# A hybrid layer on one core: group squares joined on VectorE, an addition moved ahead of a silu, and one page group read by two queues

## The reference, cut to what matters

```python
def _gated_group_rmsnorm(y, z, w, out_dtype):
    g = y.astype(jnp.float32) * jax.nn.silu(z.astype(jnp.float32))
    shp = g.shape
    g = g.reshape(*shp[:-1], SSD_GROUPS, D_INNER // SSD_GROUPS)
    g = g * lax.rsqrt(jnp.mean(g * g, axis=-1, keepdims=True) + RMS_EPS)
    return (g.reshape(shp) * w.astype(jnp.float32)).astype(out_dtype)
```

```python
        k_past = cache_k[layer, pt].reshape(past, KV_HEADS, hd)
        v_tail = cache_v[layer, pt[own_start // PAGE_SIZE:]].reshape(-1, KV_HEADS, hd)
```

## Time and profile before

| | us |
|---|---|
| median of 3 runs | 1838.3 (1833.46 to 1839.65) |
| the profiled execution's own time | 1838.51 |
| its span, first to last instruction | 1836.8 |
| TensorE busy | 1755.9 (96%) |
| its weight loads busy | 1620.0 (88%) |
| VectorE busy | 934.1 (51%) |
| GpSimd busy | 955.8 (52%) |
| ScalarE busy | 614.5 (33%) |
| mean granted TensorE clock | 0.981 |

### The profile page before, as it was taken

One profiled execution on the slowest core, in us unless ns is written; L12 is line 12 of the kernel. 1 busy time (PEld: TensorE's weight loads), 2 busy tenths in 40 slices (PEclk: granted clock), 3 DMA queues, 4 the chain that ended last, 5 costly groups with the idle time before them and its releaser, 6 DMA issues.

```text
span 1836.8 us, 35809 instructions
## 1 busy us (share of the span) xinstructions
PE 1755.9 (96%) x13948; PEld 1620.0 (88%) x13948; DVE 934.1 (51%) x1552; ACT 614.5 (33%) x1652; POOL 955.8 (52%) x1090
## 2 busy tenths in 40 slices
PE   6999999999999999999898999999998999999987
PEld 6888988999889999776676998779998999999987
DVE  6776677641765423666465632212246661562463
ACT  4355545422544200455343112321024430331231
POOL 4544434455443466220453634226676886776774
PEclk9999999999999999999999999999999999999998
DMA  4213222223123223111796364632221322222222
GB/s 160 70 49 105 95 83 70 99 66 118 58 95 101 79 91 125 47 47 58 254 310 209 137 195 175 224 116 95 86 81 59 92 81 81 81 81 93 80 71 107
DMA packets 53478, 198.50 MB, mean 108 GB/s; under 512 B 6353, under 2 KB 7378, under 8 KB 49746
## 3 DMA queue, kind: packets, MB, share of 16 engines
q1 hardware_dynamic: 41330, 132.83, 22.7%
q10 hardware_dynamic: 7200, 47.81, 6.9%
q0 software_dynamic: 4800, 15.73, 2.5%
HBM read 180.43 MB, written 15.92 MB: 107 GB/s over the span
## 4 chain that ended last, share of the span: by engine, by line
PE 82%; DVE 5%; ACT 4%; issue 3%; DMA 3%; POOL 2%; POOLq 0%; DVEq 0%; SPq 0%; ACTq 0%
PE dps L221 64%; PE psLE L1595 1%; DVE cout L850 1%; DMA w_raw<-wstream_dram 1%; DMA pages<-kv_pages_dram 1%; PE psY L586 1%; PE psY L1332 1%; POOL w_lo L2510 1%; PE psY L1618 1%; ACT cs_rhs L645 1%; PE psY L522 1%; PE psLE L2040 1%; PE psLE L2002 1%; PE psA L1322 1%; PE psLE L572 1%
## 5 line engine op out<-in xcount | busy, mean ns | idle before, releaser
L2510 POOL TENSOR_TENSOR w_lo<-w_raw,w_hi 128x256 fp32r<-128x256 f32 x804 | 678.1, 875 | 16.8
L2506 POOL TENSOR_SCALAR w_hi<-w_raw 128x1024 fp32r<-128x1024 f32 x201 | 219.4, 1092 | 708.8 <-PE dps L221 691.3
L221 PE MATMUL dps<-xn_hi,w_hi 128*128 128x288 f32 x2160 | 479.5, 304 | 12.8 <-DVE xn_lo L323 4.5
L221 PE MATMUL dps<-xn_lo,w_hi 128*128 128x288 f32 x2160 | 466.0, 298 | 0.0
L221 PE MATMUL dps<-xn_hi,w_lo 128*128 128x288 f32 x2160 | 465.9, 298 | 0.0
L221 PEld LDWEIGHTS dps<-xn_hi,w_hi 128*128 128x128 f32 x2160 | 353.8, 192 | 43.2 <-issue 28.6
L221 PEld LDWEIGHTS dps<-xn_lo,w_hi 128*128 128x128 f32 x2160 | 352.4, 191 | 0.0
L221 PEld LDWEIGHTS dps<-xn_hi,w_lo 128*128 128x128 f32 x2160 | 351.5, 191 | 0.0
L221 PE MATMUL dps<-y_hi,w_hi 128*128 128x288 f32 x896 | 194.2, 299 | 5.4 <-POOL w_lo L2510 5.4
L221 PE MATMUL dps<-y_lo,w_hi 128*128 128x288 f32 x896 | 193.0, 297 | 0.0
L221 PE MATMUL dps<-y_hi,w_lo 128*128 128x288 f32 x896 | 192.9, 297 | 0.0
(11 more groups left out here) (383 smaller groups left out, 2605.3 us busy)
## 6 DMA issues: line engine op xcount, KB each, us to landing
w_raw<-wstream_dram SPq DMA_DIRECT2D x217, 512.0 KB, 3.5
pages<-kv_pages_dram SPq DMA_DIRECT2D x68, 256.0 KB, 3.8
pages<-kv_pages_dram POOLq DMA_DIRECT2D x60, 256.0 KB, 4.0
st_in<-state_t_dram ACTq DMA_DIRECT2D x8, 1024.0 KB, 4.8
ssm_s_dram<-st_in ACTq DMA_DIRECT2D x8, 1024.0 KB, 5.0
kc<-mem_kt_dram ACTq DMA_DIRECT2D x4, 2048.0 KB, 7.8
vc<-mem_v_dram ACTq DMA_DIRECT2D x3, 2048.0 KB, 7.9
h_res<-x_t_dram ACTq DMA_DIRECT2D x1, 2304.0 KB, 8.8
```

Source lines behind the costliest of these rows:

```text
L221: mm = pe.matmul(dps[:, par, b, 0:cw], w, a[:, k, c0:c0 + cw], start=(k == 0 and j == 0), stop=(k == nk - 1 and j == 2))
L2506: pool.tensor_scalar(w_hi[:, par, :], w_raw[:, par, :], 1.0, 1.0, ALU.mult, ALU.mult).then_inc(w_hi_done, 1)
L2510: ins = pool.tensor_tensor(w_lo[:, par, at], w_raw[:, par, at], w_hi[:, par, at].bitcast(F32), ALU.subtract)
```

## The change

Three things are changed.

1. The ten one-column products of `pe_gsum` become five: `dve_squares_joined` on VectorE first adds the squares of the group's second 128 features to those of the first, in place. `gsq_ready` now counts two for each group. `pe_gsum` also moves behind the next group's first chunk, except in group 4, where it stays in front of the output tiles, and group 7, which has no such chunk.
2. In `dve_slot`, `dve_round` comes ahead of `dve_silu` in slots 2 to 5.
3. Page group 3 is read two pages by SP and two by GpSimd, when `pv_full` says that the last products of the prompt's attention are done, and no longer behind `sam_start`. Both read its page numbers ahead of that wait. SP's weight load for the stage's next gate tile moves ahead of it too. SP's two pages are counted on `kv_landed[8]`, which is what the counts in `pages_here` take into account.

GpSimd has two of the four reads left, behind pv_full. The diff:

```diff
--- before.py
+++ after.py
@@ -578,12 +578,11 @@
 
         def pe_gsum(pe, G):
 
-            pe.wait_ge(gsq_ready, G + 1)
+            pe.wait_ge(gsq_ready, G * 2 + 2)
             pe.wait_ge(y_free, G * 5 + 5)
             for c in range(CH + 1):
                 at = slice(c * P, c * P + P) if c < CH else slice(T - P, T)
-                for j in range(2):
-                    mm = pe.matmul(gsum[:, c:c + 1], xg_of(G)[:, j, at], ones[:, 0:1], start=(j == 0), stop=(j == 1))
+                mm = pe.matmul(gsum[:, c:c + 1], xg_of(G)[:, 0, at], ones[:, 0:1], start=True, stop=True)
             mm.then_inc(gsum_full, 1)
 
         def pe_grow(pe, G):
@@ -621,14 +620,16 @@
                         pe_round(pe, G, k - 2)
                     if k < 5:
                         pe_chunk_out(pe, G, k)
-                    else:
-                        pe_gsum(pe, G)
                     if k < 4:
                         pe_chunk(pe, G, k + 1)
+                    if k == 5 and out_tiles(G, k):
+                        pe_gsum(pe, G)
                     for m in out_tiles(G, k):
                         pe_dense(pe, MIXER_AT["out", 0, m], y_hi, y_lo, ready=counted(glo_ready, 1) if m == 0 else None)
                     if k == 5 and G < GROUPS - 1:
                         pe_chunk(pe, G + 1, 0)
+                    if k == 5 and not out_tiles(G, k):
+                        pe_gsum(pe, G)
 
 
         def act_rhs(act, G, s):
@@ -878,6 +879,12 @@
             dve.tensor_tensor(zg_of(G), yg[:], zg_of(G), ALU.mult).then_inc(gate_ready, 1)
             dve.wait_ge(gate_ready, G + 1)
 
+        def dve_squares_joined(dve, G):
+
+            dve.wait_ge(gsq_ready, G * 2 + 1)
+            xg = xg_of(G)
+            dve.tensor_tensor(xg[:, 0, :], xg[:, 0, :], xg[:, 1, :], ALU.add).then_inc(gsq_ready, 1)
+
         def dve_variance(dve, G):
             dve.wait_ge(gsum_full, G + 1)
             dve.tensor_scalar(gvar[:], gsum, EPS, None, ALU.add).then_inc(gvar_ready, 1)
@@ -940,11 +947,12 @@
             if inner:
                 if 1 <= k <= 4:
                     dve_conv(dve, link, N, k - 1)
-                if k >= 2:
-                    dve_silu(dve, N, k - 2)
             if k >= 2:
                 dve_round(dve, G, k - 2)
+                if inner:
+                    dve_silu(dve, N, k - 2)
             if k == 5:
+                dve_squares_joined(dve, G)
                 dve_variance(dve, G)
 
         def dve_mixer(dve):
@@ -1515,21 +1523,31 @@
             sem(f"own_{k}") for k in ("s", "ready", "exp", "t", "tc", "pv", "done"))
         gate1_done = sem("gate1_done")
 
-        def load_pages(dma, n):
-
+        def page_numbers(dma, n):
             _, page = nc.values_load_multi_w_load_instructions(ptab[0:1, n * 4:n * 4 + 4], engines=(dma.engine,),
                                                                min_val=0, max_val=io["kv_pages"].shape[0] - 1)
+            return page
+
+        def read_pages(dma, n, page, which, landed):
+            for k in which:
+                dma.dma_start(pages[n % DEEP][:, k, :], io["kv_pages"][bass.ds(page[k], 1), :, :].rearrange("o p f -> (o p) f")).then_inc(
+                    landed, 16)
+
+        def load_pages(dma, n):
+
+            page = page_numbers(dma, n)
             if n >= DEEP:
                 dma.wait_ge(b_vused, n - DEEP + 1)
-            for k in range(4):
-                dma.dma_start(pages[n % DEEP][:, k, :], io["kv_pages"][bass.ds(page[k], 1), :, :].rearrange("o p f -> (o p) f")).then_inc(
-                    early_in if n == 1 else kv_landed[n % (2 * DEEP)], 16)
+            read_pages(dma, n, page, range(4), early_in if n == 1 else kv_landed[n % (2 * DEEP)])
 
         def pages_here(pe, n):
             if n == 1:
                 pe.wait_ge(early_in, 16 + 64)
-            else:
-                pe.wait_ge(kv_landed[n % (2 * DEEP)], (n // (2 * DEEP) + (n % (2 * DEEP) != 1)) * 64)
+                return
+            if n == 3:
+                pe.wait_ge(kv_landed[8], 32)
+            held = {1: 64, 3: 32, 8: -32}.get(n % (2 * DEEP), 0)
+            pe.wait_ge(kv_landed[n % (2 * DEEP)], (n // (2 * DEEP) + 1) * 64 - held)
 
         def sp_pages(sp):
             sp.wait_ge(sam_start, 1)
@@ -1540,17 +1558,23 @@
             sp.wait_ge(qbd_done, KT)
             load_pages(sp, 1)
             load_pages(sp, 2)
+            load_tile(sp, n_gate1 + 2)
+            page = page_numbers(sp, 3)
+            sp.wait_ge(pv_full, KT)
+            read_pages(sp, 3, page, (0, 1), kv_landed[8])
             sp.wait_ge(sam_start, 2)
-            for n in range(2, STEPS_S, 2):
-                if n > 2:
-                    load_pages(sp, n)
+            for n in range(4, STEPS_S, 2):
+                load_pages(sp, n)
                 if n % CHUNKS == 2:
                     load_tile(sp, n_gate1 + n // CHUNKS + 2)
 
         def pool_pages(pool):
             pool.wait_ge(early_in, 16)
+            page = page_numbers(pool, 3)
+            pool.wait_ge(pv_full, KT)
+            read_pages(pool, 3, page, (2, 3), kv_landed[3])
             pool.wait_ge(sam_start, 2)
-            for n in range(3, STEPS_S, 2):
+            for n in range(5, STEPS_S, 2):
                 load_pages(pool, n)
                 if n % CHUNKS == 1 and n < STEPS_S - CHUNKS:
                     split_tile(pool, n_gate1 + n // CHUNKS + 1)
```

## The result

The changed kernel takes 1843.4 us (median of 14 runs, 1839.8 to 1849.8) against 1836.0 (14 runs, 1830.1 to 1840.9) of the kernel before in the same shared runs: ratio 1.0047, 95% interval 1.0033 to 1.0061. It is slower by about half a per cent, as forecast (1844.2). The profiled execution took 1841.6 us (span 1839.9); before it was 1838.5 (1836.8).

A forecast was written before the change was run, and what follows sets the result against it. TensorE, 82% of the chain, was taken to bound the kernel. Ends +12.0, L510 -7.6, clock +4.5 and pages -3.0 gave +5.9 us on the profiled 1838.5, 0.2 above the median: 1844.2; 8-in-10 range 1826 to 1857.

The forecast's parts named there:

- The ends of groups: Mixer, eight group ends: chunk and sums wait for silu and join, dense work starts later; +12.0 us at full clock.
- the joining addition: VectorE at group 0's end: the join starts at 143.1, stands behind a GpSimd piece until 143.75, ends at 144.5.
- The norm's factors: After the sums: variance, root and next group's factors move along, priced at nothing; a miss adds some 0.5 us per group.
- Who gets in first: Silu at a group's end: VectorE gets the first part, GpSimd gets in ahead of the second, which takes 0.74 us.
- L510, -7.6: Slots 2 and 3: with the addition ahead of the silu, all 14 TensorE waits for it go; -7.6 us.
- The clock: Group ends: longer quiet parts lose 19.8 us to the lower clock instead of 15.3; +4.5 us.
- 0.72 at most ends: Sign: the granted clock in 12 us from a group's end should be 0.72 at most ends.
- The page group: Page group 3: earlier reads shorten TensorE's wait, though GpSimd's first read again starts 4.65 us late; -3.0 us.
- Rival 1: The main forecast: all terms as summed, 1844 us, own range 1838 to 1850; chance 0.40.
- Rivals 3 and 4: Group ends: 3, silu runs through unhindered, 1824 us, chance 0.14; 4, GpSimd first, larger falls at every end, 1857, 0.22.
- Rival 2: Clock falls as often as before, GpSimd's first read costs nothing when asked for earlier; 1835 us, chance 0.19.
- Rival 5: Slots 2 and 3: the waits of L510 stay because VectorE itself is late; 1852 us, chance 0.05.

The follow-up runs named there:

- e4: Changed kernel with silu and join ahead of the addition in slot 5; 1805.3 us, ratio 0.9845 against the kernel before.
- e1: Kernel before with only the join and five sums, old orders of TensorE and VectorE kept; 1840.5 us, ratio 1.0045.
- e6: Changed kernel without GpSimd's low parts of the weights (w_lo) for tiles 8 to 63 of the mixer; 1827.0 us, ratio 0.9955 against the kernel before.
- e9: e4 plus GpSimd's small early read of the page table, as in e8; 1799.9 us, ratio 0.9792 against the kernel before.
- e11: e4 with the sums ahead of the chunk on TensorE; 1804.5 us, ratio 0.9828 against the kernel before.
- e12: e11 plus GpSimd's small early read of the page table; 1797.5 us, ratio 0.9793 against the kernel before.
- e5: Changed kernel with two dense steps between state products and chunk at the six ends with a chunk; 1823.3 us, ratio 0.9929 against the kernel before.
- e8: Changed kernel with GpSimd reading the 512-byte page table once more, some 28 us before its first page read; 1842.3 us, ratio 1.0040 against the kernel before.
- e7: Changed kernel with SP reading all four pages of group 3, GpSimd starting with group 5; 1844.8 us, ratio 1.0060 against the kernel before.
- e3: Kernel before with only the early reads of page group 3 by both queues; 1831.5 us, ratio 0.9987.
- e2: Kernel before with only the swap, addition ahead of silu in slots 2 to 5, ten sums ahead of the chunk; 1822.8 us, ratio 0.9944.
- e10: e4 without the join, ten products in the sums again; 1825.2 us, ratio 0.9931 against the kernel before.

## Why the prediction was right, point by point

The direction and the place were right, and the time was 1844.2 against 1843.4. That it came so near is in part luck. The forecast was +5.9 us on a kernel before of 1838.3 (3 runs); measured were +7.4 on one of 1836.0 (14 runs), so the base lay 2.3 us lower and the change was 1.5 us larger. Every size in the sum was somewhat off too, and the errors cancel in part.

**The ends of groups, +12.0; measured +9.9.** The chunk starts 2.92 us after the last dense product, 2.99 by the prediction. The wait of L499 is 2.1 us, six times (2.2 was expected), that of group 4's sums 3.34 (3.6). The dense tile is 1.2 us later than before at six ends, not 1.5, 2.2 in group 4 and 0.5 in group 7. What was off is the step "the joining addition ... stands behind a GpSimd piece until 143.75, and ends at 144.5". The join did meet a GpSimd piece, and took 1.19 us instead of 0.76. But that piece ended (141.90) 0.62 us before the join did, where the prediction put the join's whole 0.77 us behind it: the join ended 4.08 us after the last dense product, not 4.3. At the six ends it holds the sums by only 0.1 us (0.33 from L513 to them, 0.23 in e4). There it isn't the join that costs but the silu in front of it; e1 shows the join's own price, with the sums first. The norm's factors, priced at nothing, cost nothing: TensorE's table of waits has no line for `pe_grow`.

**Who gets in first.** VectorE had the silu's first part (0.68), and GpSimd came between it and the second (0.74), as the prediction took from the earlier trace rows. From start to end the silu then took 1.34 us (its two durations add up to 1.42, with the small overlap counted twice) instead of the 0.81 that the same two parts take in e6. This is a measured cause: leave out the `w_lo` pieces, and the silu's second part and the join are short. The Trainium skill (SBUF — State Buffer, "SBUF: two separate sides") calls it a lock held for a whole instruction. The traces agree with that. GpSimd's four pieces, 0.72 to 0.74 us each in e4, took 1.21, 0.72, 1.24 and 0.73 here: the first stood behind the silu's first part, and the third behind the join. The silu's second part, whose work is 0.21 us, ended at 141.29, just behind the first piece (141.22). L924, which has one input in PSUM, took its 0.69 us in all 32 slots, here beside `w_hi`.

**L510, -7.6; measured -10.9.** This is the term that was off by most. All 14 waits went. But the idle time of 0.5 us counts from the modelled end of L502. Without the wait L510 starts 0.03 us after L502 does, inside it, so the wait held up some 0.75 us from product to product. Over the 14 slots the time from dense product to dense product fell from 4.46 to 3.71 us (10.9 in all, one of them at the lower clock).

**The clock, +4.5; measured +6.8.** 22.2 us lost instead of 15.4. The number of falls was well guessed, all eight; their size wasn't: half have the smaller one ("0.72 at most ends" was wrong). Against that stand group 3's end, where the clock was already down when the chunk began, and group 7's, which lost 3.4 where it had lost nothing. The prediction had it only as a bound that the loss goes to nothing; another order of the same work reaches it. In e4, e9, e11 and e12 the clock never fell in the mixer: 15 us against the kernel before, 22 against the changed one, more than any other term. e5 shows the same from the other side: dense products in the gap, no fall there.

**The page group, -3.0; measured -1.9.** The wait fell from 5.79 to 3.90. Both numbers of the step were off, in opposite directions. GpSimd's first read came 3.45 us behind its MOVE instead of 4.65. But the last page came 5.65 us after GpSimd had issued its reads (878.12 to 883.77), not 3.24. SP had issued two reads of group 3 and four of group 4 between 873.5 and 877.8. In e8 it issued the same six, but GpSimd's two were issued ahead of group 4's, and the last of them landed 4.1 us after. So the late start seems to cost a second time, behind SP's reads; no run takes these away alone. e7 and e8 bear out the main claim, that the delay belongs to GpSimd's first read and moves with it; e6 is the exception (last section).

**The sum.** From the first chunk to the last dense product of group 7 it was 544.6 us before and is 546.4 after, +1.9. The terms give the same: seven ends +9.4, L510 -10.9, clock +3.4. Group 7's end adds 0.5 and its fall 3.4, the page stage takes 2.0 off (first scores to those of the last step: 127.4 to 125.4), and the stages outside of these differ by a few us either way. In total +3.1 of span. The medians differ by 7.4. Had the profiled execution of before lost to the clock what e3's lost with the same mixer, 10.2 and not 15.4, the spans would differ by 8.2: the accounting's clock term carries an uncertainty of some 5 us, and the forecast's 0.8 us from the median is luck within that.

**Rivals.** Rival 1 came about. Rivals 3 and 4 fall by the same rows: the silu took 1.34 us, neither the 0.8 of two free parts nor the 2.2 that two held ones took in the earlier trace rows (121.22 to 123.43). Rival 2 fails on both counts, the falls (eight, not six) and the first read. Rival 5 had nothing to it. Of the signs that were to show it, two missed, the silu's "over 1.4 us" (1.34 from start to end) and 0.72 at most ends, and two were near: 3.90 us for the page wait (3) and 3.45 for the first read (4.7). One thing in the text misleads: "At a group's end the same swap turns round" reads as if the swap itself cost there. e2 shows that with the sums first it does not; the wait of L499 came with the chunk ahead of the sums.

## What to carry to other kernels

When two engines' orders are both changed, check each new order against the other's old one: here the swap alone won 0.6% and the join alone lost 0.4%, but the whole change, with the sums behind the chunk, was 0.7% worse than its parts, and moving the silu and the join in one slot made it 1.6% faster than the kernel before. Put what another engine waits for ahead of what only waits itself: silu and join had all their inputs while VectorE idled for the state products. And size a stall from product to product, not from the idle column, when products overlap.

## What the runs showed of the hardware

- **Small edits decided whether the clock fell at an end.** With 1.9 to 3.2 us between dense products and five one-column products in them, none of 32 ends fell (e4, e9, e11, e12). With ten, ends of 3.0 us (groups 4 and 7 of before, e2, e3 and e10) fell 4 times in 8, and e10's of 4.4 us 5 times in 6. With five again but 3.5 to 4.6 us (e1, where the sums wait), 6 ends of 8 fell, and with 4.2 to 5.3 us (after) all eight. So the length alone doesn't sort these ends, and the number of one-column products alone doesn't either. The ends of 3.0 us have no chunk in them and those of e4 and e11 have, so which of the differences counts stays open. Taking out 1.1 us of one-column products was worth 9 us of products and, by the traces of e10 and e4, 12 of clock.
- **GpSimd's first transfer starts late.** Only e8, e9 and e12 have a transfer of GpSimd ahead of its first page read. In ten of the other eleven kernels that read starts 3.1 to 4.7 us behind its MOVE (before 4.7, after 3.45, e3 3.1, e4 3.8, e7 3.1). In e8, e9 and e12, with a 512-byte read 29 to 32 us before, it is 0.6. These 29 us hold no transfer either, so a pause without transfers isn't the cause. The Trainium skill (GPSIMD Engine Reference, "2.1 Instruction dispatch") has some 6 us for the first call of a freshly loaded routine; no run here shows that this is the cause. Against a plain "first transfer" speaks e6, where the delay was 0.7 us without any early read. There GpSimd had made 124 `w_lo` pieces before instead of 348, though the last of them was as recent as in the others (29 us). Each kernel has one trace, so chance isn't ruled out for e6. The cause stays open.
- **A small operation pays a big one's price.** The 128x64 part of the silu, 0.21 us of work, took 0.74 to 0.76 in 30 of the changed kernel's 32 silus, where a GpSimd piece came between; the 128x512 part in front of it took its own 0.68 or 0.69 in 30 of 32. It looks as if splitting the operation gave the other engine an opening; no run here has the silu in one piece.
